# Second half of the context network: gate and up slabs split into two parts, down slabs kept in plain fp32, and the first gathered dot later in the order

## The chip, the cores and the metric

The kernel runs on one core of one Trainium2 chip. The metric is the device time of one execution in microseconds, taken as the median over runs. A core has five engines that run side by side and wait for each other through semaphores: TensorE (PE: matmuls; PEld is its weight load), VectorE (DVE), ScalarE (ACT), GpSimd (POOL) and SyncE (SP), which here only issues transfers.

## The reference

The program is two transformer blocks behind each other in fp32. Block one has a delta-rule branch, a dilated attention and a mixture of single experts ("peer"): for every token 8 x 16 experts are chosen by two rounds of top-16, and out = sum over the chosen of gelu(u_e . x) * gate * v_e. Block two (two layers) works on 512 latent tokens, with a context of 256 tokens whose first layer has a gated network of its own. What the change touches is that network, for the context of layer 0:

```
h   = rms_norm(ctx) * (1 + scale) + shift        # 256 tokens x 1024
g,u = h @ w_gate, h @ w_up                       # 1024 x 2816 each, 22 slabs of 128 columns each
ctx = ctx + gate_mod * ((silu(g) * u) @ w_down)  # 2816 x 1024
```

and the experts:

```
act = gelu(einsum('tkd,td->tk', expert_u[eb], xb))
out = einsum('tk,tkd->td', act * gb, expert_v[eb])
```

Of the 512 tokens the kernel does 384 densely (matmuls over all 16384 experts with a mostly zero gate matrix) and 128 by gathering the rows of the chosen experts, one per partition.

## The kernel before

**Slabs.** All large weights are cut into slabs of 128 x 1024 fp32 (512 KB) and stand in one list, `spine`. SP loads slab i into `raw[i % 4]` (L514). A split slab is turned by ACT into a rounded part `whi` (L522) and by DVE or POOL into the rest `wlo` (L530, with `lo` of the unit naming the engine), and PE does three matmuls a k-block in fp32r: hi x hi (L598), hi x lo of the data (L600), lo x hi (L609). There are 3 `whi` and 3 `wlo` buffers. A direct slab is not split: PE reads `raw` and the unsplit data in plain fp32 (L555, and L573 where two slabs are done in turn), one matmul a k-block, which the trace records as two instructions each.

**The context network** `cnet` is two halves. A half is 11 gate and 11 up slabs in turn, then 11 down slabs. ACT takes silu of a gate slab into `f10sg` (L3111), DVE multiplies the up slab with it into `f10w` (L3127), the down slabs read `f10w`, and DVE adds their output into `xct` (L3150). In the kernel before all 66 slabs are direct. Their data are the normed context `hct_plain`, made on DVE (L764) and shifted on ACT (L731). After `cnet` come a norm of the context (L672 to L706), its split into `hchi` and `hclo`, and the 13 slabs of the context's mixer of layer 1 (`cm1`), whose first two are done as a pair (L628, L630, L635). Then come the 128 `peer_u` and 128 `peer_v` slabs.

**Side streams.** Beside the slabs run streams whose steps a planner (`Weave`) places between the slabs' matmuls by modelled clocks, when the program is built; each engine then runs its list in order. `route` chooses the experts. `dense` has 96 steps and builds the gate matrix: DVE compares (L3458, `onehot`), ACT (L3469) or POOL (L3486), in turn, multiplies the gates in, PE multiplies (L3443) two steps later, ACT copies out to `stage` (L3477), SP stores to `gate_dram` (L3494), and slabs of it come back as `gin` (L3518). `ffn1b` makes and transposes the experts' input (L764, L735, L753, L3192). `experts` is the gathered part: POOL issues 256 indirect loads into 5 buffers `fetched` (L3646), DVE does a dot with `xtok` for each of 128 rows of u (L3604) and then a sum for each of 128 rows of v (L3618); the stream has a step each 3.96 us of the planner's time. The first gather waits until the store of the context's results (`ctx_res`, L2414) has landed, since its buffers lie on top of them. At the end of the peer slabs the stream is drained and PE transposes `xtok` (L3593).

Of the kernel before, what the change touches and what calls it, by code (L numbers as in the profile page):

```python
# [16 lines left out]
TC = 256  # L17
# [405 lines left out]
def program(nc, io):  # L423
# [284 lines left out]
    class Apply:  # L708
# [3 lines left out]
        def __init__(self, name, nm, use, pairs, gain, shift=None, late=(), once=False, before=None, eps=EPS, tap=None,  # L712
                     root=True, plain=False):
            self.only = plain
            self.name, self.nm, self.use, self.gain, self.shift, self.late = name, nm, use, gain, shift, late
            self.once, self.before, self.eps, self.tap, self.root = once, before, eps, tap, root
            self.pairs = [Pair(p.hi, p.lo, ("apply_a", name, "moved" if plain else "hi", c), self.lower_sig(c), p.plain)
                          for c, p in enumerate(pairs)]

        def lower_sig(self, c):  # L720
            return ("apply_g" if self.once and c < 3 else "apply_v", self.name, "lo", c)

        def scalar(self, a):
# [4 lines left out]
            for c, p in enumerate(self.pairs):  # L728
                a.wait_ge("apply_v", self.name, "made", c)
                if self.only:  # L730
# [13 lines left out]
                if not self.once and (c < KC - 1 or self.tap):  # L744
                    yield

# [12 lines left out]
        def vector(self, v):  # L759
# [11 lines left out]
            for c in [] if self.only else range(3, KC) if self.once else [KC - 1]:  # L771
                self.lower_vector(v, c)

        def gpsimd(self, g):
            if self.once:
                for c in range(0 if self.only else 3):
# [2291 lines left out]
    class Network:  # L3068


        def __init__(self, l, v, n, pairs, places, ring, lo, free, direct=()):
            self.l, self.v, self.n, self.free, nm = l, v, n, free, f"f{v}{l}"
            self.name, self.direct = nm, direct
            self.whole = [sb(f"{nm}w{k}", places[2 * k], [n])[:] for k in range(HALF)] if "down" in direct else None
            self.hid = [[sb(f"{nm}h{k}{y}", places[2 * k + y], [n], F32R)[:] for y in range(2)] for k in range(HALF)]
            self.sg = [sb(f"{nm}sg{i}", places[2 * HALF + i], [n])[:] for i in range(2)]
            self.taken = "lo" if v and not self.whole else "up"
            self.units = []
            for half in range(2):
                for k in range(HALF * half, HALF * half + HALF):  # L3080
                    for kind, w in (("fgate", "w_gate2"), ("fup", "w_up2")):
                        u = Unit(kind, (self, k), io[w][l * 22 + k], n, [Group(pairs, (self, k))], ring, lo[half])
                        u.frees = (lambda out: [("ffn_a", out[0].name, "gate", out[1])]) if kind == "fgate" else \
                            (lambda out: [("ffn_v", out[0].name, out[0].taken, out[1])])
                        u.direct = "up" in direct
                        self.units.append(u)
                for s in range(HALF):
                    groups = []
                    for b in range(8 * s, 8 * s + 8):
# [3 lines left out]
                        if self.whole:  # L3093
                            groups[-1].pairs.append(Pair(None, None, ("ffn_v", nm, "up", HALF * half + k), None, self.whole[k]))
# [490 lines left out]
    def expert_tensor(t):  # L3585
        for i in range(257):
            yield Every(3.96)
# [752 lines left out]
```

## Time and profile before

| | |
|---|---|
| median of 3 runs | 3975.88 us (3972.86 to 3977.01) |
| the profiled execution | 3978.74 us, its span 3976.9 us |
| PE busy | 3823.1 us (96% of the span) |
| DVE, ACT, POOL busy | 2328.4, 1570.5, 693.6 us |
| mean granted TensorE clock | 0.983 |

A row of a timeline gives start, duration, engine, line, operation and tiles; in brackets the idle time of the engine before it and who ended it. Busy times of PE overlap, since ends of matmuls are modelled: its pace is read from one start to the next. Where the text gives a time without more, it is in us from the span's start.

### The profile page before, as it was taken

How to read it: one execution, taken by the hardware profiler on the slowest of the kernel's cores; microseconds unless marked ns; L12 is line 12 of the kernel's file. 1: busy time of each engine (PE TensorE's matmuls, PEld its weight loads, DVE VectorE, ACT ScalarE, POOL GpSimd, SP SyncE). 2: the span in 40 equal slices, each digit the busy share in tenths (PEclk: the TensorE clock that was granted, in tenths of full speed). 3: DMA queues.
4: the chain of work that ended last, by engine and by line, in shares of the span. 5: the costliest groups of instructions: out<-in, count | busy, mean ns of one | idle time of the engine just before them, and what ended most of it. 6: DMA issues, size and time to landing. Idle time of an engine off the chain costs nothing.

```text
span 3976.9 us, 55816 instructions
## 1 busy us (share of the span) xinstructions
PE 3823.1 (96%) x22529; PEld 3304.4 (83%) x22529; DVE 2328.4 (59%) x4053; ACT 1570.5 (39%) x2531; POOL 693.6 (17%) x586
## 2 busy tenths in 40 slices
PE   8999999989999989999999999998899999889998
PEld 5788776778899889999999999786677777667887
DVE  6455333546888467777777776557633345664333
ACT  4523342444345543333333333536522233564222
POOL 0112000244112343222233221201100010101000
PEclk9999999999999999999999999998999999999999
DMA  5211235533355678888888886312234342203332
GB/s 207 81 41 44 102 118 200 177 99 99 108 176 198 212 238 294 289 277 284 274 283 283 285 285 196 113 55 62 82 118 136 122 143 69 74 26 87 99 97 75
DMA packets 209184, 617.19 MB, mean 155 GB/s; under 512 B 18464, under 2 KB 68640, under 8 KB 205088
## 3 DMA queue, kind: packets, MB, share of 16 engines
q1 hardware_dynamic: 168352, 465.76, 36.6%
q0 software_dynamic: 40576, 147.87, 10.8%
q8 instruction: 179, 2.93, 0.3%
q14 instruction: 77, 0.63, 0.1%
HBM read 583.67 MB, written 29.88 MB: 154 GB/s over the span
## 4 chain that ended last, share of the span: by engine, by line
PE 85%; DVE 7%; ACT 4%; DMA 2%; issue 2%; POOL 0%; SPq 0%; DVEq 0%; ACTq 0%; POOLq 0%
PE ps L598 22%; PE ps L609 21%; PE ps L600 21%; PE ps L555 6%; PE ps L3443 2%; PE ps L2513 1%; DMA raw<-w_in 1%; PE ps L2540 1%; PE ps L887 1%; DVE hlo_plain L764 1%; ACT whi L522 1%; PE ps L2121 1%; PE ps L2531 1%; PE ps L1218 1%; PE ps L1209 1%
## 5 line engine op out<-in xcount | busy, mean ns | idle before, releaser
L598 PE MATMUL ps<-hhi,whi 128*128 128x512 f32 (+1 forms) x2824 | 1075.9, 381 | 6.8 <-DVE xres L3049 2.9
L600 PE MATMUL ps<-hlo,whi 128*128 128x512 f32 (+1 forms) x2824 | 1048.8, 371 | 0.1
L530 DVE TENSOR_TENSOR wlo<-raw,whi 128x1024 fp32r<-128x1024 f32 x543 | 671.3, 1237 | 635.6 <-ACT whi L522 628.2
L522 ACT ACTIVATE whi<-raw 128x1024 fp32r<-128x1024 f32 x594 | 625.7, 1054 | 601.7 <-PE ps L609 452.8
L609 PE MATMUL ps<-hhi,wlo 128*128 128x512 f32 (+1 forms) x2824 | 670.3, 376 | 9.0 <-DVE wlo L530 9.0
L598 PEld LDWEIGHTS ps<-hhi,whi 128*128 128x128 f32 x2824 | 532.9, 189 | 108.6 <-issue 25.4
L600 PEld LDWEIGHTS ps<-hlo,whi 128*128 128x128 f32 x2824 | 533.3, 189 | 68.8 <-issue 4.1
L609 PEld LDWEIGHTS ps<-hhi,wlo 128*128 128x128 f32 x2824 | 513.2, 189 | 83.7 <-DVE wlo L530 9.4
L600 PE MATMUL ps<-ag_lo,whi 128*128 128x384 f32 x1024 | 342.0, 334 | 0.0
L598 PE MATMUL ps<-ag_hi,whi 128*128 128x384 f32 x1024 | 342.0, 334 | 0.0
L3646 POOL DMA_INDIRECT fetched<-peer_v_rows,rows x128 | 151.3, 1182 | 359.9 <-DVE xtok L3618 335.7
L3646 POOL DMA_INDIRECT fetched<-peer_u_rows,rows x128 | 153.1, 1196 | 342.4 <-DVE ract L3604 325.5
L3530 ACT ACTIVATE uact<-ps 128x384 f32<-128x384 f32 x128 | 62.9, 491 | 362.0 <-PE ps L609 361.9
L609 PE MATMUL ps<-ag_hi,wlo 128*128 128x384 f32 x1024 | 198.2, 334 | 0.0
L600 PEld LDWEIGHTS ps<-ag_lo,whi 128*128 128x128 f32 x1024 | 192.3, 188 | 0.0
L598 PEld LDWEIGHTS ps<-ag_hi,whi 128*128 128x128 f32 x1024 | 192.2, 188 | 0.0
L609 PEld LDWEIGHTS ps<-ag_hi,wlo 128*128 128x128 f32 x1024 | 179.3, 188 | 0.0
L3604 DVE CUSTOM_DVE_ANT_0 fetched<-fetched,xtok 128x1024 f32<-128x1024 f32 x128 | 156.0, 1218 | 17.3 <-DMA fetched<-peer_u_rows,rows 17.3
L3618 DVE SCALAR_TENSOR_TENSOR xtok<-fetched,ract,xtok 128x1024 f32<-128x1024 f32 x127 | 162.4, 1279 | 0.0
L3547 DVE TENSOR_TENSOR uact<-uact,gin 128x384 f32<-128x384 f32 x128 | 71.4, 558 | 151.4 <-ACT uact L3530 146.0
L555 PE MATMUL ps<-hct_plain,raw 128*128 128x256 f32 x672 | 157.6, 379 | 0.0
L683 POOL COPY nacc<-nsq 128x512 f32<-128x512 f32 x6 | 3.7, 611 | 851.3 <-ACT nsq L672 851.3
(652 smaller groups left out, 6018.7 us busy)
## 6 DMA issues: line engine op xcount, KB each, us to landing
raw<-w_in SPq DMA_DIRECT2D x151, 512.0 KB
raw<-peer_u SPq DMA_DIRECT2D x128, 512.0 KB
raw<-peer_v SPq DMA_DIRECT2D x128, 512.0 KB
raw<-w_mod SPq DMA_DIRECT2D x96, 512.0 KB
raw<-w_gate SPq DMA_DIRECT2D x66, 512.0 KB
raw<-w_up SPq DMA_DIRECT2D x66, 512.0 KB
raw<-w_down SPq DMA_DIRECT2D x66, 512.0 KB
gate_dram<-stage SPq DMA_DIRECT2D x24, 1024.0 KB, 4.3
```

Of the source, the lines that this page charges most:

```text
L522: a.x.activation(whi[n % NW][:], raw[i % NRAW][:], ACT.Copy, bias=0.0, scale=1.0).then_inc(*a.gives("hi", i))
L530: e.x.tensor_tensor(wlo[n % NW][:], raw[i % NRAW][:], whi[n % NW][:].bitcast(F32), ALU.subtract).then_inc(*e.gives(*lo_sig(i)))
L555: ins = t.x.matmul(o, w[:, 128 * (first + k):128 * (first + k) + 128], p.plain, start=grp.opens and k == 0, stop=grp.closes and k == len(g ...
L598: t.x.matmul(o, w, p.hi, start=grp.opens and k == 0, stop=False)
L600: t.x.matmul(o, w, p.lo, start=False, stop=False)
L609: ins = t.x.matmul(o, lo[:, 128 * (starts[gi] + k):128 * (starts[gi] + k) + 128], p.hi, start=False, stop=grp.closes and k == len(grp.pair ...
L3443: ins = t.x.matmul(four(b, x), ea[n % 4][:, x, :], eb[n % 4][:, x, :], start=True, stop=True)
L3530: a.x.activation(uact[j % 2][:], held(("out", "peer_u", j))[:, 0:TD], ACT.Gelu_apprx_tanh, bias=0.0, scale=1.0).then_inc(*a.gives("peer_a" ...
L3547: v.x.tensor_tensor(t3, t3, gin[g % 2][:, :, jj, :], ALU.mult).then_inc(*v.gives("peer_v", "gated", j))
L3604: v.x.tensor_tensor_reduce(c[:], c[:], xtok[:], 1.0, 0.0, ALU.mult, ALU.add, ract[:, i:i + 1]).then_inc(*v.gives("expert_v", "dot", i))
L3618: v.x.scalar_tensor_tensor(xtok[:], c[:], ract[:, i:i + 1], xtok[:], ALU.mult, ALU.add).then_inc(*v.gives("expert_v", "sum", i))
L3646: g.x.indirect_dma_start(fetched[i % NF][:], None, io["peer_v_rows" if i >= 128 else "peer_u_rows"], bass.IndirectOffsetOnAxis(ap=rows[:, ...
```

## The change

The first half of `cnet` stays as it was. In its second half the 22 gate and up slabs are no longer direct: they are split, their `wlo` is made by POOL, and their data are `hchi` and a new set of eight tiles `c0apart` for the lower part. `hchi` is made by eight more copies on ACT and `c0apart` by eight subtractions on POOL, behind the norm ahead of `cnet`. The down slabs of both halves stay direct; their input is now called `f10plain`. In the `experts` stream one step of 14 us of the planner's time stands ahead of the first dot, on all engines; the issue of the first four gathers is where it was.

```diff
@@ class Apply @@
-                     root=True, plain=False):
-            self.only = plain
+                     root=True, apart=None):
+            self.apart = apart
...
-            self.pairs = [Pair(p.hi, p.lo, ("apply_a", name, "moved" if plain else "hi", c), self.lower_sig(c), p.plain)
+            self.pairs = [Pair(p.hi, apart[c] if apart else p.lo, ("apply_a", name, "hi", c), self.lower_sig(c), p.plain)
                           for c, p in enumerate(pairs)]
+            self.whole = [Pair(None, None, ("apply_a", name, "moved", c), None, p.plain) for c, p in enumerate(pairs)]
...
+            for c, p in enumerate(self.pairs if self.apart else []):
+                a.wait_ge("apply_a", self.name, "moved", c)
+                a.x.activation(p.hi, p.plain, ACT.Copy, bias=0.0, scale=1.0).then_inc(*a.gives("apply_a", self.name, "hi", c))
...
         def gpsimd(self, g):
-            if self.once:
-                for c in range(0 if self.only else 3):
+            if self.apart:
+                g.wait_ge("apply_v", self.name, "made", KC - 1)
+                g.wait_ge("route_t", "scores", 15)
+                for c, p in enumerate(self.pairs):
+                    g.wait_ge("apply_a", self.name, "hi", c)
+                    g.x.tensor_tensor(p.lo, p.plain, p.hi.bitcast(F32), ALU.subtract).then_inc(
+                        *g.gives("apply_g", self.name, "lo", c))
+            elif self.once:
+                for c in range(3):
@@ class Network @@
-        def __init__(self, l, v, n, pairs, places, ring, lo, free, direct=()):
+        def __init__(self, l, v, n, pairs, places, ring, lo, free, whole=None):
...
-                        u = Unit(kind, (self, k), io[w][l * 22 + k], n, [Group(pairs, (self, k))], ring, lo[half])
+                        u = Unit(kind, (self, k), io[w][l * 22 + k], n, [Group(whole if self.direct and half == 0 else pairs, (self, k))],
+                                 ring, lo[half])
+                        u.direct = self.direct and half == 0
...
-                        u.direct = "up" in direct
...
-                    u.direct = "down" in direct
+                    u.direct = self.direct
@@ the gathered experts @@
     def expert_tensor(t):
+        yield Every(14.0)
         for i in range(257):
             yield Every(3.96)
...
     def expert_vector(v):
+        yield
         v.wait_ge("tap_v", 7)
...
     def expert_scalar(a):
-        for i in range(128):
+        for i in range(129):
             yield
...
         for i in range(NF - 1):
             fetch(i)
+        yield
         for i in range(128):
@@ where the context network is made @@
+    c0apart = [sb(f"c0apart{c}", kb, [TC], F32R)[:] for c, kb in enumerate((121, 122, 123, 124, 134, 135, 205, 206))]
     cffn = Apply("c0ffn", cnorm, "c0ffn", HC, lambda c: amod[:, 0, 1, 1, c:c + 1], lambda c: modv(0, 1, 24 + c), once=True,
-                 plain=True, late=[mod_ready(0)], before=("apply_v", "c0mix", "made", KC - 1))
-    cnet = Network(0, 1, TC, cffn.pairs, list(range(145, 152)) + list(range(168, 185)), "clate", ("vector", "gpsimd"), [], ("up", "down"))
+                 apart=c0apart, late=[mod_ready(0)], before=("apply_v", "c0mix", "made", KC - 1))
+    cnet = Network(0, 1, TC, cffn.pairs, list(range(168, 181)), "clate", ("vector", "gpsimd"), [], cffn.whole)
```

**DVE, from the end of the context's mixer of layer 1 (`c_res` are its last results) into the peer slabs.** Before:

```order
L530 TENSOR_TENSOR wlo_70<-raw_65,whi_67 128x1024
L2400 COPY c_res<-ps 128x2x128
L530 TENSOR_TENSOR wlo_71<-raw_62,whi_68 128x1024
L2400 COPY c_res<-ps 128x2x128 x2
L2400 COPY c_res<-ps 128x256
L3604 ISA fetched_218,ract<-fetched_218,xtok 128x1024
L3604 ISA ract 128x1
L530 TENSOR_TENSOR wlo_69<-raw_63,whi_66 128x1024
L3547 TENSOR_TENSOR uact_216<-uact_216,gin_210 128x384
L3604 ISA fetched_219,ract<-fetched_219,xtok 128x1024
L3604 ISA ract 128x1
L530 TENSOR_TENSOR wlo_70<-raw_64,whi_67 128x1024
```

In the changed kernel:

```order
L530 TENSOR_TENSOR wlo_70<-raw_63,whi_67 128x1024
L3560 TENSOR_TENSOR uact_216<-uact_216,gin_210 128x384
L530 TENSOR_TENSOR wlo_71<-raw_64,whi_68 128x1024
L3563 TENSOR_TENSOR ag_lo_214<-uact_216,ag_hi_212 128x384
L3560 TENSOR_TENSOR uact_217<-uact_217,gin_210 128x384
L530 TENSOR_TENSOR wlo_69<-raw_65,whi_66 128x1024
L3563 TENSOR_TENSOR ag_lo_214<-uact_217,ag_hi_212 128x384
L3560 TENSOR_TENSOR uact_216<-uact_216,gin_210 128x384
L530 TENSOR_TENSOR wlo_70<-raw_62,whi_67 128x1024
L3563 TENSOR_TENSOR ag_lo_214<-uact_216,ag_hi_212 128x384
L3619 ISA fetched_218,ract<-fetched_218,xtok 128x1024
L3619 ISA ract 128x1
```

Ahead of the first dot on `fetched` stood two `wlo` of peer slabs; now six `wlo`, three gatings `uact` and three `ag_lo` of peer slabs stand ahead of it.

**POOL, in the gate and up slabs of the second half (`onehot` is the dense stream's gating, `wlo` the lower part of a slab).** Before:

```order
L3486 TENSOR_TENSOR onehot_205<-onehot_205,gT 128x512
L3486 TENSOR_TENSOR onehot_207<-onehot_207,gT 128x512
L3486 TENSOR_TENSOR onehot_205<-onehot_205,gT 128x512
L3486 TENSOR_TENSOR onehot_207<-onehot_207,gT 128x512
L3486 TENSOR_TENSOR onehot_205<-onehot_205,gT 128x512
```

In the changed kernel:

```order
L530 TENSOR_TENSOR wlo_69<-raw_63,whi_66 128x1024
L530 TENSOR_TENSOR wlo_70<-raw_64,whi_67 128x1024
L3499 TENSOR_TENSOR onehot_205<-onehot_205,gT 128x512
L530 TENSOR_TENSOR wlo_71<-raw_65,whi_68 128x1024
L3499 TENSOR_TENSOR onehot_207<-onehot_207,gT 128x512
L530 TENSOR_TENSOR wlo_69<-raw_62,whi_66 128x1024
L530 TENSOR_TENSOR wlo_70<-raw_63,whi_67 128x1024
L3499 TENSOR_TENSOR onehot_205<-onehot_205,gT 128x512
L530 TENSOR_TENSOR wlo_71<-raw_64,whi_68 128x1024
L530 TENSOR_TENSOR wlo_69<-raw_65,whi_66 128x1024
L530 TENSOR_TENSOR wlo_70<-raw_62,whi_67 128x1024
L3499 TENSOR_TENSOR onehot_207<-onehot_207,gT 128x512
```

Between the gatings, which were alone on POOL, there are now 22 subtractions of 128x1024.

**PE, at the end of `cnet` (`cnacc`, `cnsq` are the norm's sums; `hchi` with `whi` the first pair of `cm1`).** Before:

```order
L555 MATMUL ps<-f10w_258,raw_63 128x256
L555 MATMUL ps<-f10w_259,raw_63 128x256
L692 MATMUL ps<-cnacc,ones 128x256
L695 MATMUL ps<-cnsq_168,ones 128x256
L695 MATMUL ps<-cnsq_169,ones 128x256
L628 MATMUL ps<-hchi,whi_66 128x256
L630 MATMUL ps<-hchi,wlo_69 128x256
L628 MATMUL ps<-hchi,whi_67 128x256
```

In the changed kernel:

```order
L555 MATMUL ps<-f10plain_265,raw_63 128x256
L555 MATMUL ps<-f10plain_266,raw_63 128x256
L3456 MATMUL ps<-onehot_205 128x128 x4
L555 MATMUL ps<-f10plain_267,raw_63 128x256
L692 MATMUL ps<-cnacc,ones 128x256
L695 MATMUL ps<-cnsq_168,ones 128x256
L695 MATMUL ps<-cnsq_169,ones 128x256
L628 MATMUL ps<-hchi,whi_67 128x256
L630 MATMUL ps<-hchi,wlo_70 128x256
L628 MATMUL ps<-hchi,whi_68 128x256
L630 MATMUL ps<-hchi,wlo_71 128x256
L3456 MATMUL ps<-onehot_206 128x128 x4
```

Dense steps, which had all been done before the last 7 down slabs, now go on to the last of them, and two of them stand behind the norm's sums, inside the pair.

## Rows read from the trace of the kernel before

**Rows 1.** The page: busy time of each engine.

```profile
PE 3823.1 (96%) x22529; PEld 3304.4 (83%) x22529; DVE 2328.4 (59%) x4053; ACT 1570.5 (39%) x2531; POOL 693.6 (17%) x586
```

**Rows 2.** Busy times by stretch: network's second half, the stall, the time behind it.

```profile
core 0: us, PE busy (x) PEld busy (x) DVE busy (x) ACT busy (x) POOL busy (x), PEclk, DMA share, GB/s
1196.30:1321.40 125.10, 125.10 (x794) 115.58 (x793) 104.68 (x170) 74.61 (x182) 28.83 (x26) 1.00 0.60 204
1321.40:1371.20 49.80, 49.80 (x283) 45.26 (x283) 16.23 (x18) 20.81 (x48) 14.70 (x14) 1.00 0.61 201
1444.60:1453.60 9.00, 0.00 (x0) 0.00 (x0) 2.41 (x4) 0.00 (x0) 3.45 (x4) 0.79 1.04 371
1453.60:1456.50 2.90, 2.89 (x9) 2.89 (x10) 2.90 (x5) 1.85 (x3) 1.83 (x2) 0.50 0.70 232
```

**Rows 3.** Timeline of PE, end of the network: plain fp32 and dense steps.

```profile
1343.83 1.05 PE L3443 MATMUL ps<-onehot 128*128 128x128 f32 x8
1344.72 26.50 PE L555 MATMUL ps<-f10w,raw 128*128 128x256 f32 x122
1371.06 0.59 PE L692 MATMUL ps<-cnacc,ones 128*128 128x256 f32 x2
```

**Rows 4.** Timeline of PE in the context's mixer of layer 1.

```profile
1376.35 0.55 PE L628 MATMUL ps<-hchi,whi 128*128 128x256 f32 x1 [3.41 <-ACT hchi L737]
...
1391.31 1.12 PE L609 MATMUL ps<-hchi,wlo 128*128 128x256 f32 x8
1392.27 0.28 PE L598 MATMUL ps<-hchi,whi 128*128 128x256 f32 x1
...
1401.07 0.36 PE L598 MATMUL ps<-hchi,whi 128*128 128x256 f32 x1
1401.27 0.28 PE L600 MATMUL ps<-hclo,whi 128*128 128x256 f32 x1
...
1418.65 0.38 PE L598 MATMUL ps<-hchi,whi 128*128 128x256 f32 x1 [3.37 <-ACT c_nvT L1980]
```

**Rows 5.** One line's or tile's instructions: ns min/median/max, first and last start.

```profile
L522 ACT ACTIVATE whi<-raw x594: 1038/1054/1084, 23.8 to 3947.5; 128x1024 fp32r<-128x1024 f32 x198
L530 POOL TENSOR_TENSOR wlo<-raw,whi x52: 2339/2388/2860, 771.0 to 1423.2; 128x1024 fp32r<-128x1024 f32 x52
L3486 POOL TENSOR_TENSOR onehot<-onehot,gT x48: 1040/1042/1482, 1092.4 to 1337.7; 128x512 f32<-128x512 f32 x48
L3477 ACT ACTIVATE stage<-ps x96: 574/597/600, 1096.2 to 1344.9; 128x512 f32<-128x512 f32 x96
L3458 DVE TENSOR_TENSOR onehot<-ps,iT x96: 1196/1215/1226, 1088.7 to 1336.4; 128x1024 f32<-128x1024 f32 x96
L764 DVE SCALAR_TENSOR_TENSOR hlo_plain<-xres,cst,nr x16: 734/742/2894, 784.1 to 1263.0; 128x512 f32<-128x512 f32 x16
```

**Rows 6.** Timeline of DVE, POOL and SP around the first gathered dot.

```profile
1433.48 0.42 DVE L2400 COPY c_res<-ps 128x256 f32<-128x256 f32 x1 [0.20 <-PE ps L2392]
1451.19 1.23 DVE L3604 CUSTOM_DVE_ANT_0 fetched<-fetched,xtok 128x1024 f32<-128x1024 f32 x1 [17.28 <-DMA fetched<-peer_u_rows,rows]
...
1441.70 1.05 POOL L3646 DMA_INDIRECT fetched<-peer_u_rows,rows  x1 [10.39 <-issue]
...
1433.93 0.33 SPq L2414 DMA_DIRECT2D ctx_res<-c_res  x1
1440.87 0.38 SPq L3518 DMA_DIRECT2D gin<-gate_dram  x1
```

**Rows 7.** Timeline of PE in the first peer slabs.

```profile
1440.25 1.55 PE L609 MATMUL ps<-hhi,wlo 128*128 128x384 f32 x8
1441.63 0.33 PE L598 MATMUL ps<-hhi,whi 128*128 128x384 f32 x1
...
1453.61 2.93 PE L609 MATMUL ps<-hhi,wlo 128*128 128x384 f32 x8 [9.04 <-DVE wlo L530]
1456.34 0.49 PE L598 MATMUL ps<-hhi,whi 128*128 128x384 f32 x1
```

More of the change, by code:

```diff
@@ L770, in vector @@
                         yield
-            for c in [] if self.only else range(3, KC) if self.once else [KC - 1]:
+            for c in [] if self.apart else range(3, KC) if self.once else [KC - 1]:
                 self.lower_vector(v, c)
         def gpsimd(self, g):
-            if self.once:
-                for c in range(0 if self.only else 3):
+            if self.apart:
+                g.wait_ge("apply_v", self.name, "made", KC - 1)
[6 more added lines that the diff above has]
+                for c in range(3):
                     p = self.pairs[c]
@@ L3068, in program @@
     class Network:
-        def __init__(self, l, v, n, pairs, places, ring, lo, free, direct=()):
+        def __init__(self, l, v, n, pairs, places, ring, lo, free, whole=None):
             self.l, self.v, self.n, self.free, nm = l, v, n, free, f"f{v}{l}"
[L3073 to L3077, printed above, removed]
+            self.name, self.direct = nm, whole is not None
+            inner = len(places) - 2
+            self.plain = [sb(f"{nm}plain{k}", places[k], [n])[:] for k in range(HALF)] if whole else None
+            self.hid = [[sb(f"{nm}h{k}{y}", places[2 * k + y], [n], F32R)[:] for y in range(2)] for k in range(HALF)] if not whole else None
+            self.sg = [sb(f"{nm}sg{i}", places[inner + i], [n])[:] for i in range(2)]
             self.units = []
@@ L3081, in __init__ @@
                     for kind, w in (("fgate", "w_gate2"), ("fup", "w_up2")):
-                        u = Unit(kind, (self, k), io[w][l * 22 + k], n, [Group(pairs, (self, k))], ring, lo[half])
+                        u = Unit(kind, (self, k), io[w][l * 22 + k], n, [Group(whole if self.direct and half == 0 else pairs, (self, k))],
+                                 ring, lo[half])
+                        u.direct = self.direct and half == 0
                         u.frees = (lambda out: [("ffn_a", out[0].name, "gate", out[1])]) if kind == "fgate" else \
-                            (lambda out: [("ffn_v", out[0].name, out[0].taken, out[1])])
-                        u.direct = "up" in direct
+                            (lambda out: [("ffn_v", out[0].name, "lo" if out[0].v and not out[0].direct else "up", out[1])])
                         self.units.append(u)
@@ L3107, in fgate_scalar @@
         if k >= 2:
-            a.wait_ge("ffn_v", f.name, "up" if f.whole else "lo", k - 2)
+            a.wait_ge("ffn_v", f.name, "up" if f.direct else "lo", k - 2)
         for s in f.free:
@@ L3115, in product @@
     def product(f, k):
-        return f.whole[k % HALF] if f.whole else held(("out", "fup", (f, k)))[:, 0:f.n] if f.v else f.sg[k % 2]
+        return f.plain[k % HALF] if f.direct else held(("out", "fup", (f, k)))[:, 0:f.n] if f.v else f.sg[k % 2]
     def fup_vector(v, i, phase):
@@ L3134, in fup_scalar @@
         f, k = spine[i].key
-        if phase and not f.whole:
+        if phase and not f.direct:
             a.wait_ge("ffn_v", f.name, "up", k)
```

11 lines of the change are left out of this document (5 added, 6 removed).

## The prediction

> **What bounds the kernel now.** The page comes first: PE is busy for 3823.1 of 3976.9 us [rows 1], so what shortens or stops PE's own list moves the end, and the other engines count only where PE waits for them. The change touches two places, so I asked for busy times by stretch. In the second half of the network PE is busy for all of 125.1 and all of 49.8 us, at a granted clock of 1.00, with DVE at 104.7 of 125.1 us, ACT at 74.6 and POOL at 28.8 [rows 2]. This place is bound by PE's own pace, and DVE is next. At 1444.6 the opposite is seen: 9.00 us in which PE does nothing, and then 2.9 us at a granted clock of 0.50, the lower of the two levels, after that idle time [rows 2].
>
> The timelines say why. PE's wait of 9.04 us in the third peer slab ends with a `wlo` of DVE [rows 7]. DVE had done its last `c_res` copy at 1433.9 and then stood for 17.28 us before the first dot, whose row of u had not arrived [rows 6]. The `wlo` stands behind that dot in DVE's list. POOL could issue the first gather only at 1441.70, since the store of `ctx_res`, issued at 1433.93, had to land; the load of `gin`, which waits for the same landing, goes out at 1440.87 [rows 6].
>
> **Term 1: 22 slabs from plain to split.** Plain fp32: 122 records from 1344.72 to 1371.06 are 26.34 us, 0.216 us each, and a slab has 16 of them: 3.45 us [rows 3]. Split: eight matmuls of 256 columns go from 1391.31 to 1392.27, 0.120 us each, and a slab has 24: 2.88 us [rows 4]. The saving is 22 x 0.574 = 12.6 us.
>
> Against it stands the change between kinds of matmul. Behind four plain matmuls of 128 columns the next fp32r matmul goes from 1401.07 to 1401.27, 0.20 us and not 0.12 [rows 4]. In the changed order 25 dense steps stand between split slabs of this stretch, so 25 x 0.08 = **2.0 us** are given back (bounds 0, if the 0.08 lies already in the dense step's own 0.89 us, and 4).
>
> **Term 2: what splitting costs the other engines.** The 22 new `whi` are 22 x 1.054 = 23.2 us on ACT, the 22 `wlo` 22 x 2.388 = 52.5 us on POOL [rows 5]. The planner has answered by moving dense steps: 53 stood in these 22 slabs, now 25; the 11 down slabs behind them held 14 and hold 40. A dense step is 0.89 us on PE [rows 3], 1.215 on DVE, 0.597 and more on ACT, 1.04 on POOL every second time [rows 5]. PE will need 22 x 2.88 + 25 x 0.89 + 2.0 + about 1.5 of small work = 89 us. DVE needs 104.7 - 28 x 1.215 = 71 us, ACT at most 74.6 + 23.2 - 28 x 0.597 = 81, POOL 28.8 - 14 x 1.04 + 52.5 = 67. In the down slabs PE needs 11 x 3.45 + 40 x 0.89 = 74 us, DVE 16.2 + 26 x 1.215 = 48. By sums PE stays the bound, and all this is hidden. With that cover gone each late `wlo` would cost PE what it is late by.
>
> Sums are not orders, though. One stretch is tight: the eight norm steps of `ffn1b` with eight products `hlo` on DVE, 16 operations with two inputs in SBUF, stand in about eight of these slabs, and PE transposes each of the eight results right behind. Such an operation took 742 ns at the median and up to 2894 [rows 5]; POOL's `wlo` went from 2339 to 2860. DVE's comparisons, which read one input from PSUM, stay within 1196 to 1226 all the time. POOL, busy here for 28.8 of 125 us before, will be so for 67 of 89. If three of four of the 16 meet a `wlo` in flight and wait for half of one, DVE loses 16 x 0.75 x 1.2 = 14 us in some 33 us of time, of which its own list fills about 25 (between its first and last norm step by the order), so that 8 are taken up. PE then waits in the transposes for the rest. I take **+4 us**, between 0 (no meeting) and 16 x 2.15 - 24 = +10 (all meet the longest wait, 2894 less 742 ns, and what DVE idles there and in the slabs around takes up 24). The Trainium skill, SBUF - State Buffer, section Who interferes with whom, states the mechanism: VectorE and GpSimd share a pair of ports, a VectorE operation with two inputs in SBUF cannot run beside a GpSimd operation that reads SBUF, and the second to come is blocked until the first ends. This trace agrees (the 2894 ns against 742). Without the rule the term is 0; by it, read strictly, it is the +4 to +10.
>
> **Term 3: new steps behind the norm ahead of the network.** Eight copies on ACT stand ahead of the first silu, eight subtractions on POOL ahead of its first gating. PE's first pair of direct slabs is 32 records, 6.9 us at 0.216 [rows 3], and the first `onehot` on POOL starts only at 1092.4 [rows 5]. Both are covered: 0.
>
> **Term 4: two dense steps moved behind the norm.** They leave 2 x 0.89 = 1.8 us of PE ahead of the norm of `c1mix` and enter the pair, where PE waits anyway (3.41 us for ACT's `hchi`) [rows 4]. ACT's and POOL's last dense work now stands close ahead of the norm's chain, though, and can delay it. **-1.0**, between -1.8 and +1.
>
> **Term 5: the mixer of layer 1.** By the order, the second group of `c_tmp` matmuls stands one slab earlier. PE's wait there is now 3.37 us [rows 4]; it would wait longer, with that slab's work left to do behind it. **+0.4**, between -2 and +3 (a slab).
>
> **Term 6: the first dot.** Ahead of it now stand the `wlo` of six peer slabs. The third slab's tail goes on at 1445 in the times of before, and the dot is reached near 1448.3 (third slab's end 1446.0, then silu, gating, `ag_hi` and `ag_lo`, some 2.3 us). Its row still lands no earlier than 1451.2 [rows 6], so DVE still waits, some 3 us. What stands behind is late next: a gating, and the `wlo` of the seventh slab. A slab is 24 matmuls of (1441.63 - 1440.25) / 8 = 0.173 us, 4.15 us [rows 7]. The seventh slab starts at 1458.5 and wants its `wlo` at 1461.3; DVE is there by 1455. ACT's silu of the fifth slab, whose bank the seventh takes, waits behind the same gating, until about 1456. So 2.5 to 6 us of late landing are covered. SP's loads behind the wait for `ctx_res` are free at 1441, and the seventh slab's load has 16 us to land. PE's wait disappears: -9.04; and so does the half clock behind it, where eight matmuls took from 1453.61 to 1456.34, 2.73 instead of 1.38: -1.35 [rows 7]. **-10.4** (bound: -4, if the rows land some 6 us later because weight loads now run beside the gathers).
>
> **At the end of the peer slabs** the last sum stands directly ahead of the transposes; DVE has a quarter of its time free there, so 0. PE has no wait in the slabs between, so what is gained at 1445 stays gained.
>
> **Sum.** -12.6 + 2.0 + 4 - 1.0 + 0.4 - 10.4 = -17.6 us. Against the profiled execution's own 3978.74 us this is 3961.1. That one lies 2.9 us above the median of the runs, 3975.88, so for the median: **3958 us**.
>
> **The rivals.**
> *A, the gathers land late.* With weight loads, `gin` and five gathers after 1441 together, DVE's new wait outlasts the cover, and PE stops at the seventh slab. For it: DMA share was 1.04 at 371 GB/s in the stall already [rows 2]. Against: 16 us of cover for the load, 3 to 6 for the dot. Term 6 is -4: 3965 us.
> *B, the shared ports decide.* Term 2 is +10 to +14 and eats the split's gain of 12.6 less 2.0; only the first dot's gain is left: 3964 to 3968, at 3966 us. The page named above would have it so if nearly every one of the 16 met a `wlo`; comparisons and products with PSUM inputs, the bulk of DVE's work, speak against it.
> *C, the other side: POOL's order.* In POOL's list a `wlo` stands behind each gating, which waits for DVE's comparison. If these waits make each of the 22 `wlo` late by more than PE's lead, PE stops in every slab and its clock falls after the stops. It decides from 17.6 / 22 = 0.8 us a slab on; at 2 us a slab the kernel takes 3958 + 44 - 4 = 3998 us, at 1.2 us 3984. Against: POOL would be busy for 3.0 of 4.0 us a slab, and `wlo` is made two slabs ahead.
> *D, more than forecast.* No contention, the dense steps in the pair wholly hidden: and the change between kinds of matmul inside the dense step's own time: terms 1, 2 and 4 at their lower bounds, 3958 - 2.0 - 4 - 0.8 = 3951 us.
>
> **Chances.** Forecast 0.60 (its own range 3953 to 3963), A 0.10, B 0.14, C 0.05, D 0.11. The range reaches to D and over A and most of B: 3947 to 3969. A measurement of this kernel tells 0.2%, 8 us, from no change: faster means under 3968. Faster 0.60 + 0.10 + 0.11 + 0.10 of B = 0.91; same 0.04 of B and little else, 0.04; slower C, 0.05.
>
> **What would show it.** Term 1: L609 matmuls on `hchi` in the second half, 24 starts in 2.9 us, and the stretch from its first slab to the norm's sums 174.8 - 12.6 + 2.0 - 1.8 + 4 = 166 us. Term 2: L764 and L753 rows over 2 us there, and PE waits that end with DVE's `hlo_plain`. Term 6: no PE wait over 1 us in the first eight peer slabs, the granted clock at 1.00, and a DVE wait of 2 to 8 us before the first dot. The forecast is wrong if PE waits for POOL's `wlo` in many slabs, or if a new wait of PE stands at the fourth to eighth peer slab.

## The result and the profile after

| | before | after |
|---|---|---|
| median | 3975.88 us (3972.86 to 3980.54, 11 runs) | 3964.32 us (3958.91 to 3969.86, 11 runs) |
| span of the profiled execution | 3976.9 us | 3961.4 us |

The ratio is 0.9968 with a 95 % interval of 0.996 to 0.9976: faster by 0.32 %, 11.6 us between the medians. A later set of runs of the same kernel gave 0.9961 (0.9947 to 0.9974). The forecast of 3958 us was 6 us too low, inside its range, and its sign was right. Behind that stand two costs that were too small, by 4 and by 3 us, and a cost of 2 us that was not there; what is left of the 6 us is no more than the scatter of the medians.

The busy times on the page of the changed kernel, which answer to [rows 1]:

```profile
PE 3809.4 (96%) x22705; PEld 3297.4 (83%) x22705; DVE 2350.0 (59%) x4053; ACT 1591.9 (40%) x2561; POOL 749.8 (19%) x616
```

Next, the busy times by stretch of the changed kernel: the gate and up slabs of the network's second half, its down slabs with the norm's sums, the mixture up to the first peer slab, and the nine peer slabs that stand ahead of the first slab of v. The columns are those of [rows 2].

```profile
1191.10:1286.20 95.10, 90.67 (x745) 88.97 (x744) 91.39 (x148) 60.72 (x120) 64.56 (x33) 0.98 0.59 196
1286.20:1359.30 73.10, 73.10 (x492) 68.55 (x492) 49.80 (x47) 50.81 (x130) 28.57 (x28) 1.00 0.60 216
1359.30:1426.50 67.20, 54.74 (x393) 51.96 (x392) 34.09 (x55) 37.03 (x63) 31.20 (x18) 0.92 0.50 161
1426.50:1464.00 37.50, 37.50 (x218) 37.50 (x218) 26.32 (x38) 17.11 (x26) 11.89 (x11) 1.00 0.92 334
```

What the reader is to see: the stall of [rows 2] is gone from the last row, PE is busy for all of it at a granted clock of 1.00. In the first row PE is no longer busy throughout, as it was before; it stands for 4.4 of 95.1 us, and VectorE is busy for 91.39 us, where the forecast had given it 71.

**Where the time went, by stretch.** All times are from the start of one matmul to the start of another, where the kind of matmul changes, read from PE's timeline. "Norm" is the time from the last down slab's last matmul to the norm's last matmul on `cnacc`, "mixture" (the rest of the norm and the context's mixer of layer 1) from there to the first peer slab, "peers" from there to the first slab of v, which stands nine slabs later.

| kernel | first half | gate and up | down | norm | mixture | peers |
|---|---|---|---|---|---|---|
| before | 142.40 | 125.31 | 49.39 | 0.43 | 61.93 | 48.28 |
| after | 142.39 | 95.36 | 72.61 | 0.43 | 67.25 | 37.53 |
| after, second profile | 142.12 | 95.37 | 72.62 | 0.43 | 64.57 | 37.53 |
| move of the dot alone | 143.67 | 125.31 | 49.39 | 0.43 | 60.36 | 37.53 |
| network alone | 143.57 | 95.36 | 72.62 | 0.43 | 65.73 | 47.16 |
| dense ahead of the norm | 142.26 | 95.35 | 72.62 | 2.39 | 62.43 | 37.56 |
| dot two slabs earlier | 142.36 | 95.36 | 72.61 | 0.43 | 67.21 | 38.96 |
| low halves by memset | 142.29 | 87.49 | 72.62 | 0.43 | 65.53 | 37.55 |
| ten more slabs split | 132.26 | 94.09 | 75.29 | 0.43 | 69.46 | 37.53 |
| ten more, and the row | 132.53 | 94.07 | 75.29 | 9.55 | 60.13 | 37.53 |
| low halves on VectorE | 142.75 | 76.98 | 66.24 | 0.43 | 84.46 | 47.34 |
| on VectorE, and the row | 142.74 | 76.97 | 66.24 | 25.78 | 62.53 | 37.56 |
| both engines, and the row | 143.77 | 84.65 | 71.05 | 14.58 | 61.61 | 37.56 |

The gate and up slabs and the down slabs repeat within 0.02 us from one execution to the next where the order is the same. The mixture does not: 67.25 and 64.57 us in two profiles of one kernel. Nor does code that nothing touched: the network starts at 1053.74 us before and between 1048.40 and 1053.98 in the other twelve profiles, and the part behind the first slab of v lasts 2495.4 to 2500.5 us. That is why the 15.5 us between the first two spans are not all the change's (5.24 of them lie ahead of the network), and why stretches are compared here and not spans.

### The profile page after: what moved, and what is told of

Same layout as the page of the kernel before. It is cut to its first block, busy times and chain, and to the rows that moved or that the text cites. A ratio compares the mean times of both kernels' runs of the same rounds, so it can differ in the third digit from the quotient of the medians.

```text
span 3961.4 us, 56261 instructions
## 1 busy us (share of the span) xinstructions
PE 3809.4 (96%) x22705; PEld 3297.4 (83%) x22705; DVE 2350.0 (59%) x4053; ACT 1591.9 (40%) x2561; POOL 749.8 (19%) x616
## 4 chain that ended last, share of the span: by engine, by line
PE 84%; DVE 8%; ACT 4%; DMA 2%; issue 2%; POOL 0%; SPq 0%; DVEq 0%; ACTq 0%; POOLq 0%
PE ps L598 22%; PE ps L609 22%; PE ps L600 21%; PE ps L555 4%; PE ps L3456 2%; PE ps L2524 1%; DVE hlo_plain L768 1%; DMA raw<-w_in 1%; PE ps L898 1%; PE ps L2551 1%; ACT whi L522 1%; PE ps L2542 1%; PE ps L2132 1%; PE ps L1229 1%; PE ps L1220 1%
## 5 line engine op out<-in xcount | busy, mean ns | idle before, releaser
L522 ACT ACTIVATE whi<-raw 128x1024 fp32r<-128x1024 f32 x616 | 649.1, 1055 | 600.0 <-PE ps L609 457.7
L530 POOL TENSOR_TENSOR wlo<-raw,whi 128x1024 fp32r<-128x1024 f32 x74 | 180.9, 2454 | 167.8 <-ACT whi L522 158.4
```

The lines of the kernel that those rows point to most:

```text
L522: a.x.activation(whi[n % NW][:], raw[i % NRAW][:], ACT.Copy, bias=0.0, scale=1.0).then_inc(*a.gives("hi", i))
L530: e.x.tensor_tensor(wlo[n % NW][:], raw[i % NRAW][:], whi[n % NW][:].bitcast(F32), ALU.subtract).then_inc(*e.gives(*lo_sig(i)))
```

## The experiments

**1. The move of the first dot alone.** In the kernel before, only the experts' stream is given its late step:

```diff
     def expert_tensor(t):
+        yield Every(14.0)
     def expert_vector(v):
+        yield
```

(and a `yield` on ScalarE and GpSimd.)

> The kernel before with the move of the first gathered dot alone (the network's slabs as they were). Theory 1 (the two parts of the change add up, and the move is worth the wait that it removes): 10.4 to 10.8 us less than before, about 3965 us, ratio 0.9973; no wait of TensorE above 1 us in the first eight peer slabs. Rival (the move pays only together with the network, because its gathers and the context's load meet the same stretch at a different time): less than 6 us gained, 3970 us or more.

Measured: 3966.22 us (3959.45 to 3968.3), before beside it 3977.86, ratio 0.9969 (0.9958 to 0.998). The peers take 37.53 us and not 48.28: 10.75 less. Theory 1 holds. VectorE's timeline in this kernel, at the first dot:

```profile
1447.01 1.23 DVE L3606 CUSTOM_DVE_ANT_0 fetched<-fetched,xtok 128x1024 f32<-128x1024 f32 x1 [2.52 <-DMA fetched<-peer_u_rows,rows]
```

VectorE still waits, for 2.52 us, and no wait of TensorE follows. The forecast had some 3 us.

**2. The network alone.** The changed kernel without those lines.

> The changed kernel with the first gathered dot put back where it stood before (the network part alone). Theory 1 (the network gives 6.7 us, and the stretch from the norm to the first peer slab gives 5.3 of them back): 1 to 2 us less than before, about 3974.5 us, ratio 0.9996. Rival (the prediction's own terms: network 7.6 less, first mixture 0.4 more): about 7 us less than before, 3969 us, ratio 0.998. By both the wait of TensorE at the first peer slab comes back, by 9 us or a little less.

Measured: 3974.8 us (3971.43 to 3979.82), ratio 0.9991 (0.9982 to 1.0). The median is theory 1's. The interval takes in no gain at all, and its lower end lies where the prediction's own terms (7.2 us less, 0.9982) would be, so these runs don't rule them out; the stretches do. From the network's start to the first slab of v this kernel takes 424.9 us and the kernel before 427.7, 2.9 less. TensorE's wait at the peer slabs is back, with 6.6 us, and the peers take 47.16 us. Most of the measured gain is the dot's: 10.75 of the 13.0 us that the stretches give.

**3. Two dense steps forced ahead of the norm.** The planner is told to finish the dense stream's multiplications first:

```diff
     run(len(cnet.units) - 2)
+    plan.need("dense multiplied")
     summed("c1mix")
```

> The changed kernel with the last two dense steps forced ahead of the norm, so that the order of work from the norm to the first peer slab is that of the kernel before. Theory 1 (the 5.3 us lost between the norm and the first peer slab come from the order: two dense steps inside the pair at half clock, and the second split of the mixture standing one slab earlier): that loss shrinks to under 2 us, the kernel takes 3960 to 961 us, 3 to 5 us less than the changed kernel, ratio to before 0.996. Rival (the loss comes from how far VectorE and ScalarE lag behind when the norm is reached, whatever the order): the same as the changed kernel within 1.5 us, 3963 to 3966 us.

Measured: 3964.18 us (3958.78 to 3967.76), ratio 0.9966 (0.9954 to 0.9977): the same as the changed kernel. The stretches say why no more was to be seen. Norm and mixture together take 64.82 us, against 67.68 and 65.00 in the two profiles of the changed kernel, so 0.2 to 2.9 us are won, less than the medians can tell. The median is the rival's. The stretches go theory 1's way, but not as far: against the 62.36 us of the kernel before, 5.3 us were lost in the changed kernel's first profile and 2.5 are lost here, not under 2. The wait that the order makes did change. TensorE's waits by releaser in the mixture, first of the changed kernel, then of this one:

```profile
PE ps L598 <- ACT c_res L1991: 4.9, 1, 4.9
PE ps L628 <- ACT hchi L738: 3.4, 1, 3.4
PE ps L635 <- DVE hclo L760: 1.9, 1, 1.9
PE ps L2119 <- DVE c_tmp L2297: 1.5, 1, 1.5
PE ps L2403 <- ACT c_svT L1991: 0.6, 1, 0.6
```

```profile
PE ps L598 <- ACT c_nvT L1991: 3.5, 1, 3.5
PE ps L628 <- ACT hchi L738: 3.4, 1, 3.4
PE ps L2119 <- DVE c_tmp L2297: 1.5, 1, 1.5
PE ps L635 <- DVE hclo L760: 1.3, 1, 1.3
PE ps L2403 <- DVE c_res L2411: 0.3, 1, 0.3
```

The wait behind the second group of `c_tmp` is 4.9 us in five profiles with the changed order (two of the changed kernel, experiments 2, 4 and 5) and 3.4 to 3.5 in the three with the old one (the kernel before, experiment 1 and this one). The wait for `hclo` follows no order: 0.5 us before, 1.9 and 0.4 after, 1.5 in experiment 1, none in experiment 2. It seems to trade with the clock. Up to PE's first matmul on `c_gvT` (an input of the mixer's own) the mean granted clock was 0.76 before and 0.88 in experiment 1, and both took 14.4 us from the last down slab: at the lower clock TensorE would come to the place later and wait less.

**4. The dot two slabs earlier.** `Every(14.0)` becomes `Every(7.0)`.

> The changed kernel with the first gathered dot moved by half as much, so that it stands behind the low halves of peer slabs 0 to 3. Theory 1 (the gathers land at a fixed time, about 16 us behind the first peer slab's start, and TensorE's cover is 3 to 6 us): VectorE waits 5 to 8 us in front of the dot, TensorE 1 to 4 us behind it, and the kernel takes 1 to 4 us more than the changed kernel, 3965 to 3968 us. Rival (any place behind the loads is as good, the slabs ahead of the dot cover it): within 1 us of the changed kernel.

Measured: 3965.72 us (3962.84 to 3977.39), ratio 0.9975 (0.9964 to 0.9985). The medians don't part it from the changed kernel; the timelines do, and they are theory 1's. VectorE at the first dot, in the changed kernel and in this one, and then TensorE in this one:

```profile
1442.78 1.22 DVE L3619 CUSTOM_DVE_ANT_0 fetched<-fetched,xtok 128x1024 f32<-128x1024 f32 x1 [0.20 <-DMA fetched<-peer_u_rows,rows]
```

```profile
1442.76 1.22 DVE L3619 CUSTOM_DVE_ANT_0 fetched<-fetched,xtok 128x1024 f32<-128x1024 f32 x1 [7.64 <-DMA fetched<-peer_u_rows,rows]
```

```profile
1445.45 0.45 PE L598 MATMUL ps<-hhi,whi 128*128 128x384 f32 x1 [1.15 <-ACT uact L3543]
```

The row lands at the same time in both. A wait of 7.64 us on VectorE costs TensorE 1.15 us (and the peers 38.96 - 37.53 = 1.43), so some 6.5 us of it were covered; the forecast had 2.5 to 6 for a dot two slabs later. The wait comes where the forecast looked for it: ScalarE's silu, which has to free a bank, stands behind the same gating of VectorE.

**5. The hold-ups between GpSimd and VectorE.** GpSimd writes the 22 new low halves as zeros (the lines stand under a condition that picks these slabs). This leaves the low halves of these weights out of the computation:

```diff
+            e.x.memset(wlo[n % NW][:].bitcast(F32), 0.0).then_inc(*e.gives(*lo_sig(i)))
+            return
```

> The changed kernel with the low halves that GpSimd makes for the second half of the network written as zeros by a memset, in the same place of its list: the low halves of those 22 weights are left out of the computation, everything else stands in the same order. A memset reads nothing from SBUF. Theory 1 (VectorE's long operations with two inputs in SBUF are held up by GpSimd's subtractions): VectorE's 16 operations of the norm and its products, 26.2 us in the changed kernel, fall back to 13 us, its busy time in the gate and up slabs from 91.4 to about 74 us, the waits of TensorE there (4.2 us in all) fall under 1.5 us, and the kernel takes 3 to 4 us less, about 3961 us. Rival (TensorE's waits there come from the order of VectorE's list and not from GpSimd): the same waits, the same time within 1.5 us.

Measured: 3958.26 us (3950.29 to 3958.86), ratio 0.9947 (0.9934 to 0.9961), and the gate and up slabs take 87.49 us and not 95.36: 7.87 less, twice what theory 1 expected. The same stretch of this kernel, and of its VectorE the comparisons and the groups of the stream `ffn1b`; then such groups in the changed kernel and in the kernel before (columns: busy us, mean ns of one, idle before):

```profile
1196.30:1283.80 87.50, 87.50 (x747) 87.47 (x746) 71.99 (x143) 61.00 (x120) 32.93 (x33) 1.00 0.63 214
```

```profile
L3474 DVE TENSOR_TENSOR onehot<-ps,iT 128x1024 f32<-128x1024 f32 x27 | 32.9, 1220 | 5.9 <-PE ps L3459 5.4
L771 DVE SCALAR_TENSOR_TENSOR hlo_plain<-xres,cst,nr 128x512 f32<-128x512 f32 x8 | 6.9, 862 | 0.0
L760 DVE TENSOR_TENSOR hlo<-hlo_plain,hhi 128x512 fp32r<-128x512 f32 x8 | 6.1, 764 | 0.0
```

```profile
L3471 DVE TENSOR_TENSOR onehot<-ps,iT 128x1024 f32<-128x1024 f32 x27 | 32.6, 1212 | 2.7 <-PE ps L3456 2.3
L757 DVE TENSOR_TENSOR hlo<-hlo_plain,hhi 128x512 fp32r<-128x512 f32 x8 | 16.1, 2018 | 0.0
L768 DVE SCALAR_TENSOR_TENSOR hlo_plain<-xres,cst,nr 128x512 f32<-128x512 f32 x8 | 10.1, 1263 | 0.0
...
L3376 DVE TENSOR_TENSOR rank<-rank,rank 128x128 f32<-128x128 f32 x1 | 2.4, 2427 | 0.0
L3365 DVE SCALAR_TENSOR_TENSOR rank<-su,rank 128x128 f32<-128x128 uint32 x1 | 2.4, 2397 | 0.0
```

```profile
L753 DVE TENSOR_TENSOR hlo<-hlo_plain,hhi 128x512 fp32r<-128x512 f32 x8 | 7.2, 904 | 0.0
L764 DVE SCALAR_TENSOR_TENSOR hlo_plain<-xres,cst,nr 128x512 f32<-128x512 f32 x8 | 5.9, 738 | 0.0
```

The 16 operations with two inputs in SBUF take 13.1 us before, 26.2 us after and 13.0 us here. The comparisons, which read one input from PSUM, take 1212 to 1220 ns in all of them. The 13.0 us here still hold three meetings with GpSimd's gatings. The memset itself holds up nothing: two of the 16 operations stood wholly inside one and took 742 and 745 ns. The first of them, below GpSimd's row:

```profile
1243.16 0.95 POOL L531 MEMSET wlo<- 128x1024 f32 x1 [1.23 <-ACT whi L522]
1243.20 0.74 DVE L771 SCALAR_TENSOR_TENSOR hlo_plain<-xres,cst,nr 128x512 f32<-128x512 f32 x1
```

Also held up in the changed kernel are small operations of the stream `route`, 2.4 us for 128 x 128 elements, which take 0.29 us in this kernel. TensorE waits behind the held-up operations, as its waits by releaser in the changed kernel's gate and up slabs say (4.2 us in all):

```profile
PE ps L3205 <- DVE xtok L3209: 2.8, 2, 1.8
PE ps L3205 <- DVE hlo_plain L768: 0.7, 1, 0.7
PE ps L3456 <- ACT stage L3490: 0.5, 2, 0.3
PE ps L609 <- POOL wlo L530: 0.2, 1, 0.2
```

Behind the longest of these waits it also runs slower:

```profile
1249.40:1254.40 5.00, 5.00 (x29) 4.92 (x30) 5.00 (x5) 2.36 (x5) 3.51 (x2) 0.66 0.46 130
```

The granted clock is 0.66 there, and 1.00 in the rest of the stretch. The matmuls from 1249.37 to 1254.33 take 4.96 us, and the same ones in this kernel 3.33 (1251.05 to 1254.38): the lower clock costs 1.6 us. The other 6.2 of the 7.87 us come at the waits. The profile shows only 4.4 us of them as idle (95.36 less 90.93), since a matmul that ends ahead of a wait is drawn longer than the pace at which the next would follow.

**6. Ten more slabs split**, the last five gate and up pairs of the first half:

```diff
-                        u.direct = self.direct and half == 0
+                        u.direct = self.direct and k < 6
```

with their `wlo` on GpSimd.

> The changed kernel with the last ten of the 22 gate and up slabs of the network's first half split too, their low halves on GpSimd. Theory 1 (a split slab is worth 0.574 us of TensorE wherever the other engines have room, and VectorE has it there less than TensorE does): 10 x 0.574 = 5.7 us less in the network, less 0.8 for the changes between kinds of matmul, 1 to 2 given back in the first mixture, where seven dense steps now stand: 3961 us, 2.5 to 4 us less than the changed kernel. Rival (VectorE is full already, 35 of 40 us in that stretch, and the dense steps that must move away from it cost as much as is won): 3964 us or more.

Measured: 3960.97 us (3957.53 to 3965.68), ratio 0.996 (0.9946 to 0.9974). The median is the one expected, but the interval holds the changed kernel's 0.9961 too. By the table the way from the network's start to the first peer slab is 371.5 us, against 378.0 and 375.1 in the two profiles of the changed kernel: 3.6 to 6.5 less. The first half gives 10.1 us: 5.7 of the ten split slabs (10 x 0.574) and 5 x 0.89 of five dense steps that now stand farther back.

**7. The same, with all dense steps in a row ahead of the norm**, by the line of experiment 3.

> As the kernel with ten more slabs split, with all dense steps forced ahead of the norm of the first mixture, eight of them in a row. Theory 1 (eight dense steps in a row go at VectorE's and the other engines' pace, 1.2 us and more each, and TensorE has nothing else to do): TensorE waits 3 to 8 us in the row, the mixture behind it is as short as in the kernel before, and the sum is 1 to 5 us worse than without the forcing, 3963 to 3966 us. Rival (the waits of the mixture are what costs, as with two dense steps forced ahead): 3959 us.

Measured: 3957.9 us (3952.93 to 3963.83), ratio 0.9952 (0.9939 to 0.9966). Theory 1 was wrong in its size: TensorE was to wait 3 to 8 us in the row and waits 1.1. The median is nearer to the rival's 3959, but not for the rival's reason. The row and the mixture of this kernel:

```profile
1350.29:1359.84 9.55, 8.37 (x67) 7.75 (x66) 6.19 (x6) 7.70 (x22) 3.34 (x4) 1.00 0.92 338
1359.84:1419.97 60.13, 51.38 (x378) 48.95 (x377) 31.20 (x54) 36.06 (x60) 32.86 (x17) 0.94 0.48 156
```

Eight dense steps in a row take 9.55 us, 1.19 each (0.89 on PE's own account). The mixture is 9.3 us shorter. Together 69.7 us, as in experiment 6 (69.9): in a row or strewn through the mixture, a dense step costs TensorE the same. The medians of 6 and 7 lie 3 us apart; of their profiles, 2.7 us lie behind the first slab of v, where the order is the same.

**8. Low halves on VectorE**, `("vector", "vector")` for the network.

> The changed kernel with the low halves of the second half's 22 gate and up slabs on VectorE, not on GpSimd. Theory 1 (VectorE's own work, 91.4 us less the 18 us in which GpSimd held it up, and 22 x 1.22 us more, makes 100 us where TensorE needs 91): TensorE waits for VectorE in these slabs, or the dense steps move into the mixture behind; 8 to 15 us more than the changed kernel, about 3975 us. Rival (without the hold-ups VectorE has room for its own low halves, and GpSimd was the wrong place): 3964 us or less.

Measured: 3967.78 us (3962.75 to 3973.28), ratio 0.9976 (0.9965 to 0.9986). Neither theory had it right. VectorE is busy for 70.6 us of 76.98 and TensorE does not wait, but 11 of the 26 dense steps, 13.4 us of VectorE's comparisons, are pushed out of the stretch; that there was room for the low halves and these too is not shown. From the network's start to the first peer slab it is 370.9 us, 4 to 7 less than in the changed kernel. The loss is behind that. The last dense steps now stand right ahead of the peers, in VectorE's list and in SP's:

```profile
1439.86 0.56 DVE L3560 TENSOR_TENSOR uact<-uact,gin 128x384 f32<-128x384 f32 x1 [15.91 <-DMA gin<-gate_dram]
```

```profile
1441.40 0.69 PE L598 MATMUL ps<-hhi,whi 128*128 128x384 f32 x1 [7.88 <-ACT uact L3543]
```

```profile
1426.69 9.10 SPq L3531 DMA_DIRECT2D gin<-gate_dram  x2
```

These are VectorE, TensorE and SP's queue in the first peer slabs. The first gating needs `gin`, and SP's row of its two loads lasts from 1426.69 to 1435.8. VectorE waits 15.91 us, TensorE 7.88.

**9. On VectorE, with the row ahead of the norm.**

> The kernel with the low halves on VectorE, and all dense steps forced ahead of the norm of the first mixture, 22 of them in a row. Theory 1 (in the kernel with the low halves on VectorE the way from the network's start to the first peer slab was 7.2 us shorter than in the changed kernel, and the loss of 9.8 us behind it came from the last dense steps, whose stored result the peers' gates are loaded from): the first peer slabs take 37.5 us again, the mixture without dense steps 60 us and the row 22 x 1.19 = 26 us; from the network's start to the first peer slab 142.4 + 77.0 + 66.2 - 4 + 26 + 60 = 368 us, 10 us less than in the changed kernel: 3954 us. Rival (a row of 22 dense steps at VectorE's pace costs more than the waits it does away with): 3962 us or more.

Measured: 3961.39 us (3959.0 to 3966.87), ratio 0.9959 (0.9945 to 0.9972). Its parts came as theory 1 had them, except for the sum: peers 37.56 us, the row 25.78. Yet from the network's start to the first peer slab it is 374.3 us and not 368. The 4 us that I had taken off had no ground, and the mixture took 62.5 and not 60. The median lies 7 us above theory 1's 3954 and at the rival's 3962.

**10. Gate slabs on VectorE, up slabs on GpSimd, and the row.**

> The changed kernel with the low halves of the second half's gate slabs on VectorE and those of the up slabs on GpSimd, and all dense steps forced ahead of the norm. Theory 1 (the loss by hold-ups, 7.9 us with 22 subtractions on GpSimd, is about half with 11, and VectorE has room for 11 x 1.22 = 13.4 us in place of the 18 us in which it was held up): 3 to 5 us less than the changed kernel, 3960 us. Rival (VectorE is as full as before and dense steps move into the row ahead of the norm): 3963 us or more.

Measured: 3963.01 us (3960.7 to 3967.62), ratio 0.9964 (0.995 to 0.9977). To the first peer slab 375.7 us: the rival. Twelve dense steps had moved into the row.

**11. The changed kernel again**, beside the last two.

> The changed kernel again, unedited, beside the two others on the same chip: 3964 us, and a second profile of it that shows how far its stretches repeat. Both theories expect its gate and up slabs of the second half within 0.1 us of 95.4 us, the down slabs within 0.1 us of 72.6, and the mixture between 66 and 68 us.

Measured: 3961.41 us (3958.25 to 3966.94), ratio 0.9961 (0.9947 to 0.9974). Gate, up and down slabs repeat within 0.01 us. The mixture was expected between 66 and 68 us and took less: with the norm's 0.43 it is 65.00 us, where the first profile had 67.68. From `c_gvT` on the two have the same list of waits; the first ran at mean granted clocks of 0.97, 0.93 and 0.88 in the three parts behind it, this one at 1.00, 0.93 and 0.97.

No version stands clear of the changed kernel. The ratios of 0.9952 (experiment 7), 0.9959, 0.996 and 0.9961 (the changed kernel again) have intervals that overlap.

## Why the prediction was right, and where its terms were off

Each measured term is after less before, from the table; for the mixture it is the mean over kernels of one order, since single profiles differ by 2.7 us.

| term | forecast | measured |
|---|---|---|
| 1: split, with the changes between kinds | -12.6 + 2.0 | -12.8 |
| 2: hold-ups on VectorE and what TensorE pays behind them | +4 | +7.9 |
| 3: steps ahead of the network | 0 | 0 |
| 4 and 5: two dense steps moved, mixture | -1.0 + 0.4 | +2.7 |
| 6: first dot | -10.4 | -10.75 |
| sum | -17.6 | -13.0 |

**Term 1.** Without hold-ups (experiment 5) gate, up and down slabs take 87.49 + 72.62 = 160.1 us, against 174.7 before. That is 14.6 less, of which 2 x 0.89 = 1.8 are the dense steps that left the stretch. 12.8 remain: the 12.6 of the split were right, and the 2.0 us for the changes between kinds of matmul were not there. This was the lower bound that the prediction named, that the 0.08 us lie in the dense step's own 0.89; whether this is the reason no run here shows.

**Term 2 is the step that failed in size**, at +7.9 instead of +4, inside the bounds of 0 and +10. Its mechanism was right: operations of VectorE with two inputs in SBUF are held up by GpSimd's subtraction, and PE then waits in the transposes. The prediction's own working, 14 us lost and 8 of them taken up, gives +6; for the +4 it had no reason. The 14 us were 13.1. The 8 us of slack were 5.2: matmul for matmul PE falls 7.9 us behind experiment 5, all of it between 1236.3 and 1268.1, beside the norm steps. One cause is the stream `route`, which has operations with two SBUF inputs too. With them VectorE lost some 18 us in the stretch (busy 91.65 us against 71.98 in experiment 5, of which 1.4 us are steps that stand just ahead of the stretch there), and it came to its first norm step 45.5 us behind the stretch's start where experiment 5 has 40.1. And the lower clock behind a wait, which the prediction counted at the first dot, cost 1.6 of the 7.9 us here and was not counted. The rule of the Trainium skill, SBUF - State Buffer, section Who interferes with whom, has a part that the prediction did not use: a GpSimd instruction that only writes SBUF does not contend with a VectorE operation with two inputs. The runs agree: beside memsets of 0.95 us in place of the subtractions the 16 operations take 13.0 us, and the two that stood wholly inside a memset took 742 and 745 ns.

**Term 3** was right: the first half takes 142.40 us before and 142.39 after, with the same first wait of PE of 3.4 us.

**Terms 4 and 5 failed by 3.3 us.** The two dense steps gave 1.8 us ahead of the norm, as said. They were to be half hidden in the pair, "where PE waits anyway". They were not: that wait of 3.41 us stands ahead of the pair's first matmul, the dense step behind it, and from the pair's start to `c_gvT` it is 1364.38 to 1375.29 = 10.91 us and not 1376.35 to 1385.22 = 8.87. The second group of `c_tmp`, one slab earlier, did what the prediction named and priced too low: the wait of 3.37 us [rows 4] became 4.9. From the norm on the kernels with the new order take 67.25, 65.73, 67.21, 65.53 and 64.57 us, 66.06 at the mean; those with the old order 61.93, 60.36 and 62.43, 61.57 at the mean. The kernels of experiments 7, 9 and 10, where all dense steps stand ahead of the norm, have 60.13, 62.53 and 61.61: it is the order that matters, and not which network stands ahead of it. 4.5 less 1.8 is the +2.7. Of the 4.5 the dense steps are 1.8, the two waits 1.5 and 0.3; the 0.9 that is left lies within what the granted clock does from profile to profile, and is not settled.

**Term 6** was right in its mechanism and, with 10.75 for 10.4 us, in its size. That the prediction asked for a VectorE wait of 2 to 8 us before the dot, and the changed kernel shows 0.20, is no contradiction to its mechanism. The store of `ctx_res` landed in 5.1 us there (1427.28 to the load of `gin` at 1432.38) and in 6.9 before [rows 6]; where it took 7.2, in experiment 1, the wait was 2.52. It goes with the order of the mixture: 5.1 to 5.2 us in the changed kernel's two profiles and in experiments 2, 4, 5 and 6, and 6.9 to 7.3 in the kernel before and in experiments 1, 3, 7, 9 and 10. Why is open.

**The rivals.** A did not occur. Experiment 4 lets one estimate where it would begin: at a VectorE wait of about 6.5 us (7.64 less 1.15). B was the nearest. Its mechanism cost 7.9 us, short of its 10 to 14, but its 3966 us lies nearer to the measured 3964.3 us than the forecast of 3958 does (not to the 3961.4 of the later set), so the time alone could not have told the two apart. C did not occur: TensorE's waits for GpSimd's `wlo` come to 0.2 us. (Of its two times the second was added up wrongly: at 1.2 us a slab the first one's sum gives 3980 us and not 3984.) D fell with term 2, though its assumption on the changes between kinds was true. The sum of -13.0 us lies in the intervals of both measured gains, of 11.6 us and, in the later set of runs, 17.6. That the later set hits the forecast's 17.6 us is luck: the first set's interval (9.5 to 15.9 us) leaves it out, and the stretches show its terms off by +3.9, +3.3, -2.2 and -0.35. The stretch from the network's second half to the norm's sums, forecast at 166 us, took 168.0; there the terms 1 and 2 offset each other in part.

## What to carry to other kernels

When work goes to GpSimd, list every VectorE operation with two SBUF inputs that runs beside it, the small ones too: each can last as long as GpSimd's instruction and more. If the sum of VectorE comes near that of TensorE, count TensorE's waits at more than the idle time that the profile shows (6.2 us for 4.4 here), and add what a lower clock behind a long one costs (1.6 us here). A step that a planner moves out of a full stretch is not saved. In both orders tried here it was paid where it lands: norm and mixture take 62.0 us at the mean without a dense step, 69.9 with eight strewn through them, and 69.7 with the eight in a row ahead (8 x 0.89 = 7.1). A place at which a step is hidden in a wait was not found here. A wait for a transfer may be cured by order alone: one late step in one stream, with no added instruction, gave most of this change's gain.

## What the hardware showed that I had not expected

- GpSimd's subtraction of 128 x 1024 elements lengthened a VectorE operation on 128 x 128 elements from 0.29 to 2.4 us. The operation started 0.13 us behind the subtraction and ended 0.15 us behind its end:

```profile
1204.10 2.38 POOL L530 TENSOR_TENSOR wlo<-raw,whi 128x1024 fp32r<-128x1024 f32 x1 [0.58 <-ACT whi L522]
1204.23 2.40 DVE L3365 SCALAR_TENSOR_TENSOR rank<-su,rank 128x128 f32<-128x128 uint32 x1
```

- The same code in the same order took 64.57 and 67.25 us in two profiles of one kernel; the granted clock differed, and one wait (1.9 and 0.4 us). The down slabs, where TensorE is always busy, repeated within 0.02 us at 72.6 us, and so did the gate and up slabs at 95.4 us, with 4.4 us of idle time in them.
